# Sharing the last residual update of a four-sublayer decoder step between VectorE and GpSimd

## The reference, cut to what matters

```python
x = x + 0.5 * rmsnorm(swiglu(rmsnorm(x, norm_pre[layer, 2]), ffn_in[layer, 1], ffn_out[layer, 1]), norm_post[layer, 2])
```

## Time and profile before

| What | Value |
|---|---|
| median of 3 runs | 1502.08 us |
| the three runs | 1501.91, 1502.08, 1507.91 us |
| the profiled execution's own time | 1506.38 us |
| its span, first to last instruction | 1504.7 us |
| its granted TensorE clock, mean | 0.992 |
| VectorE busy in the last 10.7 us of the span (16 instructions) | 6.61 us |
| GpSimd busy in the same 10.7 us | 0.00 us |

### The profile page before, as it was taken

The page is one execution under the profiler, slowest core; times in us unless marked ns, Lnnn a source line. Parts: engine busy times, 40 slices in busy tenths (PEclk is TensorE's granted clock), DMA queues, the critical chain, the costliest instruction groups (busy, mean ns, idle before and its releaser), DMA issues.

```text
span 1504.7 us, 29720 instructions
## 1 busy us (share of the span) xinstructions
PE 1457.2 (97%) x11034; PEld 1370.2 (91%) x11034; DVE 909.9 (60%) x1513; ACT 745.8 (50%) x1200; POOL 142.8 (9%) x209
## 2 busy tenths in 40 slices
PE   8999998999989999999999999999999999999997
PEld 8999997999877889999989999998866688999997
DVE  5656437979877486554376555348655547656534
ACT  6555435778444365554346555345533345555432
POOL 0111000000100001110001111001043300111000
PEclk9999999999999999999999999999999999999998
DMA  6443442433331234434424434434497742443441
GB/s 234 154 157 139 153 154 92 159 128 146 111 120 50 100 102 154 163 139 147 160 84 172 162 140 146 161 140 163 143 278 244 229 162 92 169 159 139 151 156 63
DMA packets 50563, 222.62 MB, mean 148 GB/s; under 512 B 6625, under 2 KB 23138, under 8 KB 28338
## 3 DMA queue, kind: packets, MB, share of 16 engines
q1 hardware_dynamic: 39138, 191.66, 35.8%
q0 software_dynamic: 6192, 24.64, 4.9%
q10 hardware_dynamic: 5152, 5.25, 1.1%
HBM read 214.74 MB, written 6.77 MB: 147 GB/s over the span
## 4 chain that ended last, share of the span: by engine, by line
PE 84%; DVE 11%; ACT 2%; issue 2%; DMA 1%; ACTq 0%; DVEq 0%; SPq 0%
PE psum L246 14%; PE psum L247 14%; PE psum L251 14%; PE psum L334 7%; PE psum L336 7%; PE psum L335 7%; PE psum L2322 2%; PE psum L2278 2%; DVE w_lo L234 2%; DVE x L399 1%; ACT w_hi L227 1%; DVE h_lo L441 1%; DVE y L395 1%; PE psum L2155 1%; DVE ssx L436 1%
## 5 line engine op out<-in xcount | busy, mean ns | idle before, releaser
L234 DVE TENSOR_TENSOR w_lo<-raw,w_hi 128x2048 fp32r<-128x2048 f32 x163 | 379.1, 2326 | 310.2 <-ACT w_hi L227 310.1
L227 ACT ACTIVATE w_hi<-raw 128x2048 fp32r<-128x2048 f32 x158 | 302.8, 1917 | 353.4 <-PE psum L336 215.9
L246 PE MATMUL psum<-h_hi,w_hi 128*128 128x320 f32 x1520 | 451.6, 311 | 2.0 <-DVE arena L1052 1.3
L247 PE MATMUL psum<-h_lo,w_hi 128*128 128x320 f32 x1520 | 449.8, 309 | 0.0
L246 PEld LDWEIGHTS psum<-h_hi,w_hi 128*128 128x128 f32 x1520 | 286.0, 188 | 3.0 <-DVE arena L1052 1.6
L247 PEld LDWEIGHTS psum<-h_lo,w_hi 128*128 128x128 f32 x1520 | 286.1, 188 | 0.5
L251 PE MATMUL psum<-h_hi,w_lo 128*128 128x320 f32 x1520 | 254.4, 309 | 0.0
L251 PEld LDWEIGHTS psum<-h_hi,w_lo 128*128 128x128 f32 x1520 | 230.9, 188 | 0.5 <-DVE w_lo L234 0.2
L336 PE MATMUL psum<-hid_hi,w_lo 128*128 (+1 forms) x704 | 217.3, 309 | 0.0
L334 PE MATMUL psum<-hid_hi,w_hi 128*128 (+1 forms) x704 | 217.3, 309 | 0.0
L335 PE MATMUL psum<-hid_lo,w_hi 128*128 (+1 forms) x704 | 217.3, 309 | 0.0
(11 more groups left out here) (415 smaller groups left out, 1954.8 us busy)
## 6 DMA issues: line engine op xcount, KB each, us to landing
raw<-wts SPq DMA_DIRECT2D x164, 1024.0 KB, 4.8
h_plain<-cache_t POOLq DMA_DIRECT2D x44, 160.0 KB, 3.6
h_plain<-cache_t SPq DMA_DIRECT2D x44, 160.0 KB, 3.3
arena<-s POOLq DMA_DIRECT2D x4, 1024.0 KB, 6.9
sgs<-arena POOLq DMA_DIRECT2D x4, 1024.0 KB, 4.1
marena<-cache_t POOLq DMA_DIRECT2D x20, 160.0 KB, 3.7
marena<-cache_t SPq DMA_DIRECT2D x20, 160.0 KB, 3.3
raw<-cache_c SPq DMA_DIRECT2D x16, 128.0 KB, 3.9
```

Source lines behind the costliest of these rows:

```text
L227: act.activation(w_hi[c0 % 2][:, :], raw[c0 % 2][:, :], ACT.Copy).then_inc(hi_ready, 1)
L234: eng.tensor_tensor(w_lo[c0 % 2][:, :], raw[c0 % 2][:, :], w_hi[c0 % 2][:, :].bitcast(F32), ALU.subtract).then_inc(lo_ready, 1)
L246: pe.matmul(outs[n], wtile(w_hi, c0, n * K + k), src_hi(k), start=(k == 0), stop=False)
L247: pe.matmul(outs[n], wtile(w_hi, c0, n * K + k), src_lo(k), start=False, stop=False)
```

## The change

The call of `residual_dve` for stage 5 is replaced by `last_residual_dve`, and GpSimd gets `last_residual_pool` behind its last feed-forward block, ahead of its five closing waits. VectorE still does all eight scalings, and the additions of tiles 0, 2, 4 and 6. GpSimd does the additions of tiles 1, 3, 5 and 7, each when `y_scaled` shows that the tile is scaled. GpSimd counts them in `gu_ready`, which stands at 88 (`4 * HT`) after the four feed-forward blocks. The output transfers wait for both counters. VectorE's order becomes: scale 0, scale 1, add 0, scale 2, scale 3, add 2, scale 4, scale 5, add 4, scale 6, scale 7, add 6.

```diff
+        def last_residual_dve(dve):
+
+            s = 5
+
+            def scale(m):
+                dve.tensor_tensor(y[:, m, :], y[:, m, :], r_post[:, :], ALU.mult).then_inc(y_scaled, 1)
+
+            dve.wait_ge(rpost_ready, s + 1)
+            dve.wait_ge(y_copied, 3 * (s + 1))
+            dve.wait_ge(y_copied_act, 5 * (s + 1))
+            scale(0)
+            scale(1)
+            for m in range(0, KT, 2):
+                dve.wait_ge(y_scaled, KT * s + m + 1)
+                dve.tensor_tensor(x[:, m, :], x[:, m, :], y[:, m, :], ALU.add).then_inc(x_ready, 1)
+                if m + 2 < KT:
+                    scale(m + 2)
+                    scale(m + 3)
+
+        def last_residual_pool(pool):
+            for m in range(1, KT, 2):
+                pool.wait_ge(y_scaled, KT * 5 + m + 1)
+                pool.tensor_tensor(x[:, m, :], x[:, m, :], y[:, m, :], ALU.add).then_inc(gu_ready, 1)
@@ -2661,7 +2685,8 @@
             for m in range(0, KT, 2):
-                sp.wait_ge(x_ready, 5 * KT + m + 2)
+                sp.wait_ge(x_ready, 5 * KT + m // 2 + 1)
+                sp.wait_ge(gu_ready, 4 * HT + m // 2 + 1)
                 sp.dma_start(io["y_t"][:, m:m + 2, :], x[:, m:m + 2, :]).then_inc(out_done, 16)
@@ -2695,6 +2720,7 @@
             ffn_pool(pool, 3)
+            last_residual_pool(pool)
             pool.wait_ge(ss_out, 16 * NG)
@@ -2777,7 +2803,7 @@
             post_dve_sum(dve, 5, half(5))
-            residual_dve(dve, 5)
+            last_residual_dve(dve)
```

## The result

The changed kernel takes 1511.34 us in the median of 13 runs (1509.71 to 1516.98), the kernel before 1503.63 us in the median of 13 (1500.33 to 1509.3; more runs than were shown ahead of the prediction). The ratio is 1.0052, with a 95% interval of 1.0039 to 1.0065: 7.7 us or 0.5% slower. The forecast was 1503.3 us, 1.24 us slower, with a range that ended at 1507.6. The direction was right and the size was not: six times as much was lost, and the measured time lies outside the range.

The account below looks back on a forecast made before the run. The end was taken as bound by VectorE's last add, awaited by the fourth transfer. Turns of 2.92 us plus 0.15, less 0.08 and 1.60 + 0.12 saved, were put at 1.24 with rounding: 1502.08 + 1.24 = 1503.3 us, range 1500.7 to 1507.6.

Parts of the forecast that it names:

- What bounds the end: Kernel's last ten microseconds: the later add that the fourth transfer waits for sets the end, 1502.12; only its shift counts.
- GpSimd's closing: Program's end: GpSimd's five closing waits, delayed to 1503.4, are covered with 2 us by the landing at 1505.6; cost nothing.
- The turns: Last residual: VectorE and GpSimd exclude each other on SBUF inputs, 0.73 us per GpSimd add, four adds 2.92; chance 0.75.
- lower bound: Last residual: 0.67 us held per add, in proportion from a 576-element copy's 0.60; 1.00 us later in all.
- The end of the turns: Last residual's end: GpSimd's last add recorded to 1503.36, 1.24 us later; fourth transfer 7.9 us behind scale 0, not 6.67.
- The sum in terms: Last residual: 1.60 + 0.12 saved, 2.92 spent, 0.15 for GpSimd's end, less 0.08; given as 1.23 us.
- The signal from GpSimd to SP: Ahead of the fourth output transfer: taken as 0.03 us like VectorE's to SP, up to 0.28 more for the range.
- The first rival, side by side: Last residual: both engines run at once, the last add ends 1.11 us earlier, 1501.0 us; chance 0.08.
- The second, kept out: Last residual: GpSimd waits until VectorE is done, four adds then end 1.68 us later, 1503.8 us; chance 0.12.
- The third, run spread: Whole kernel's time: the shift drowns in run differences, median may be 1507.6 or above; no separate chance given.
- The chances: Whole kernel's time: faster by more than 0.5% 0.01, within it 0.97, slower by more 0.02; every case within 2.1 us.
- signs of being wrong: Last residual in the changed profile: wrong if VectorE's twelve instructions keep a pace of 0.40 us throughout.

Follow-up runs that it names:

- m1: Small program of its own, no transfers by GpSimd: VectorE additions beside GpSimd work of five kinds; losses 0.33, 0.66, 1.34 us beside additions of 160, 320, 640 elements.
- e6: Changed kernel without GpSimd's closing drain, its four additions replaced by memsets of 960 elements; no scaling above 0.494, add 6 ends 4.9 us behind scale 0.
- e4: Changed kernel with one more GpSimd drain, behind its last feed-forward multiplication and ahead of the four additions; 1505.13 us, ratio 1.0011 to the kernel before.
- e7: Kernel before with VectorE's sixteen last residual instructions made eight of two tiles, GpSimd having no part; 1501.31 us, ratio 0.9992.
- e3: Kernel before with GpSimd's closing drain left out; 1505.04 us, ratio 1.0013.
- e5: Changed kernel with GpSimd adding tile 1 alone and VectorE the other seven; one run, span ends 11.3 us behind scale 0.
- e2: Kernel before with one wait added at the end of GpSimd's program, for the last of VectorE's residual instructions; 1512.09 us, ratio 1.0057.
- e1: Changed kernel with GpSimd's closing drain left out; 1504.62 us, ratio 1.0005 to the kernel before.

## Why the prediction was wrong, step by step

- **What bounds the end.** "So the end is set by the later of the two adds that the fourth transfer waits for. All that the change can bring or cost is the shift of that one moment." This is the first half of the error. It was true of the kernel before, and it was carried over to a kernel in which another engine also works up to the end.
- **GpSimd's closing.** "GpSimd's four waits delay its five closing waits to 1503.4; these were met long ago and end ahead of the landing at 1505.6, which covers them with 2 us." This is the step that failed: it put all that GpSimd does behind its additions at nothing. The waits do pass at once, as said. Behind them stands the drain, which no step of the sum named. It measured 9.08 us where the cover was 2.4, and so cost 6.7. It was in the trace of before, from 1416.8 to 1426.3. The views that count busy instructions leave it out, and the source doesn't write it, since the block's end emits it; but the view of line L115 shows it with its 9507 ns, and L115, there on VectorE, ends the chain in the earlier trace rows.
- **The turns.** Right in mechanism, in place and in number: three scalings stretched, four additions with 1.04 us each (about 1.0 forecast), the fourth behind add 6 and wholly exposed. The size was 0.66 per turn instead of 0.73, which with four turns makes 0.27 less. By m1's line the 0.73 counted 0.07 of start-up, which lies beside VectorE's work when GpSimd has to wait. The prediction's lower bound, 0.67 by proportion from a copy, was the better value, in part by luck: m1's copy of 320 elements held the inputs for 0.25 us, and in proportion that would have given 0.50. The Trainium skill's figure for two-input operations ("GPSIMD Engine Reference", section "3.1 Elementwise — side-by-side cycle accounting") gave an estimate of 0.69, above the 0.66 measured.
- **The end of the turns.** Forecast: the fourth transfer 7.9 us behind scale 0. Measured: 7.69, against 6.67 before, so 1.02 later instead of 1.24. The sum in terms was also added up wrongly: 2.92 + 0.15 - 0.08 - 1.60 - 0.12 is 1.27, not 1.23. The 1.24 comes from the times counted through, and stands.
- **The signal from GpSimd to SP.** Taken as 0.03, measured 0.07 (1500.084 to 1500.157).
- **The first rival, side by side**, is excluded by the scalings of 1147 ns, and e6 shows what it would have looked like: an end of add 6 at 4.9 us. **The second, kept out**, is excluded by GpSimd's records, each in the gap behind an addition of VectorE. **The third, run spread**, is no account of the 7.7 us: the interval of the ratio starts at 1.0039, and the trace has the 7.68 from scale 0 on.
- **The chances.** All cases were variants of one mechanism, and so the 0.97 for "within 0.5%" rested on the claim that every case lies within 2.1 us. The measured ratio, 1.0052, lies just outside that band. A case for what a late engine does at the closing was missing, and none of the signs of being wrong looked past the fourth transfer.

The sum that would have been right, from the rows and the one record: turns and signal +1.0, less the cover, which is the 2.4 us from GpSimd's last instruction to the end of SP's closing drain, plus the drain of 9.08: 1.0 + 9.08 - 2.4 = 7.7.

## What to carry to other kernels

Before work is given to an engine that was idle at the end, look up what it still does when its program closes, in the view of the closing line or in its own records: in these runs GpSimd pays 0.082 us there for each transfer that it has issued and not yet drained, and a late wait is enough to expose it. If GpSimd has to be used late, an explicit drain in an earlier idle stretch takes that cost away (e4), but two-input VectorE work and GpSimd work that reads SBUF only take turns. An addition of 320 elements on GpSimd takes 0.66 us out of VectorE's queue, and on VectorE itself it takes 0.40, so nothing is gained in a stretch where VectorE is full. Widening the instructions of the full engine (e7) brought the fourth transfer forward by 0.67 us of 6.67, where sharing put it back by 1.02.

## What the runs showed of the hardware that wasn't expected

- GpSimd's drain costs 0.082 us per transfer issued since the last drain, for transfers of 8 KB to 1 MB that had all landed: 0.07, 0.16, 5.31 and 9.08 us for 0, 1, 64 and 110. No run has a transfer still under way at the drain. That it is a record per transfer that is worked off is inferred from the slope and from e4; no run looks inside.
- A memset on GpSimd beside VectorE's two-input work costs neither anything (0.365 us for 320 elements both beside it and alone in m1). The Trainium skill says so as well ("SBUF — State Buffer", section "Who interferes with whom": two-input VectorE work contends with what reads SBUF, not with what only writes it), and e6 agrees, with 0.486 us in the median beside memsets of 0.90.
- The start of scale 0 lies anywhere between 1489.2 and 1498.4 in the profiled executions of nine kernels that are alike up to there. It rises with the time ahead of it in which the granted TensorE clock was half (1.2 instead of 2.4 GHz): nothing in e4 (1489.25), 6.8 us in e6 (1490.82), 10.2 in e3 and e5 (1492.29 and 1492.30), 13.7 in the changed kernel (1492.47), 17.1 in the kernel before (1495.48), 23.9 in e2 and e7 (1496.96 and 1497.11) and 27.3 in e1 (1498.45). The stretches at half clock are 3.4 or 6.8 us long. In the kernel before, TensorE was busy for all of the 7.4 us ahead of the one at 315.4 us and for 5.2 of the 7.7 us ahead of the one at 499.7 us. That the clock is what moves scale 0 is read from this order alone; no run sets it. This scatter, some 9 us wide, is why differences at the end had to be read from scale 0, and why e7's 0.6 us can't be told in the times.
